# A depthwise convolution's fourth channel tile moved from TensorE to GpSimd, in a two-block transformer kernel on one core

## What is computed

```python
a, gt = jnp.split(p[..., o3:], 2, axis=-1)
u = a * jax.nn.sigmoid(gt)                        # 512 positions x 512 channels
u = _dwconv(u, w_dw_conv[l], b_dw_conv[l])        # depthwise, 31 taps along the positions, plus a bias
u = jax.nn.silu(_layernorm(u, g_conv_ln[l], b_conv_ln[l]))
y = jnp.concatenate([y_attn, u], axis=-1) @ w_o[l]
```

## Time and profile before

| | |
|---|---|
| time, median of 3 runs | 1885.44 us (1885.15 to 1885.94) |
| profiled execution, span from its first to its last instruction | 1883.8 us |
| around the span (median less span) | 1.6 us |
| busy: PE, DVE, ACT, POOL | 1861.2, 1165.4, 917.1, 75.4 us |
| granted TensorE clock, mean | 1.000 of full speed |

### The profile page before, as it was taken

One profiled execution on the slowest core, in us unless ns is written; L12 is line 12 of the kernel. 1 busy time (PEld: TensorE's weight loads), 2 busy tenths in 40 slices (PEclk: granted clock), 3 DMA queues, 4 the chain that ended last, 5 costly groups with the idle time before them and its releaser, 6 DMA issues.

```text
span 1883.8 us, 27086 instructions
## 1 busy us (share of the span) xinstructions
PE 1861.2 (99%) x8985; PEld 1504.1 (80%) x8985; DVE 1165.4 (62%) x2030; ACT 917.1 (49%) x1685; POOL 75.4 (4%) x110
## 2 busy tenths in 40 slices
PE   8999999999999999999999999999999999999998
PEld 7888888888888877677888888888757878888887
DVE  6877765733333377776566666336777576666534
ACT  6777654543433353666544434334456553444433
POOL 1111000000000000100200000000010020000000
PEclk9999999999999999999999999999999999999999
DMA  5222232333333324521333333333441223333333
GB/s 153 69 79 79 76 104 79 101 95 100 95 98 97 95 73 102 108 53 35 101 95 95 95 95 105 96 95 88 118 83 43 68 81 109 95 95 95 96 95 106
DMA packets 169241, 171.33 MB, mean 91 GB/s; under 512 B 48563, under 2 KB 123329, under 8 KB 169153
## 3 DMA queue, kind: packets, MB, share of 16 engines
q1 hardware_dynamic: 169048, 170.16, 31.5%
q10 hardware_dynamic: 104, 0.03, 0.0%
HBM read 159.25 MB, written 2.10 MB: 86 GB/s over the span
## 4 chain that ended last, share of the span: by engine, by line
PE 91%; DVE 5%; ACT 2%; issue 1%; DMA 0%; SPq 0%; DVEq 0%; ACTq 0%
PE bank_b L2457 16%; PE bank_b L2458 16%; PE bank_b L2459 16%; PE bank_a L2457 11%; PE bank_a L2458 11%; PE bank_a L2459 11%; PE bank_b L2959 2%; PE bank_b L3063 2%; PE bank_a L3044 1%; DVE w_lo L1535 1%; DVE arena L1538 1%; DVE arena L1535 1%; PE bank_a L2482 1%; PE bank_a L2485 1%; PE bank_a L2488 1%
## 5 line engine op out<-in xcount | busy, mean ns | idle before, releaser
L1535 DVE TENSOR_TENSOR w_lo<-w_raw,w_hi 128x512 fp32r<-128x512 f32 (+2 forms) x621 | 412.3, 675 | 535.3 <-ACT w_hi L1264 327.4
L1264 ACT ACTIVATE w_hi<-w_raw 128x512 fp32r<-128x512 f32 (+3 forms) x396 | 232.9, 599 | 435.6 <-PE bank_b L2459 222.2
L2457 PE MATMUL bank_b<-h_hi,w_hi 128*128 128x512 f32 (+1 forms) x952 | 372.7, 391 | 1.9 <-DVE h_lo L1538 0.8
L2459 PE MATMUL bank_b<-h_hi,w_lo 128*128 128x512 f32 (+1 forms) x952 | 369.0, 388 | 0.0
L2458 PE MATMUL bank_b<-h_lo,w_hi 128*128 128x512 f32 (+1 forms) x952 | 369.0, 388 | 0.0
L901 ACT ACTIVATE w_hi<-w_raw 128x512 fp32r<-128x512 f32 x225 | 137.7, 627 | 227.6 <-PE bank_b L2459 116.9
L2457 PEld LDWEIGHTS bank_b<-h_hi,w_hi 128*128 128x128 f32 x952 | 178.8, 188 | 41.2 <-issue 3.1
L2458 PEld LDWEIGHTS bank_b<-h_lo,w_hi 128*128 128x128 f32 x952 | 178.8, 188 | 37.0 <-issue 1.4
L2459 PEld LDWEIGHTS bank_b<-h_hi,w_lo 128*128 128x128 f32 x952 | 178.7, 188 | 36.6
L2457 PE MATMUL bank_a<-h_hi,w_hi 128*128 128x512 f32 x513 | 200.6, 391 | 0.3
L2458 PE MATMUL bank_a<-h_lo,w_hi 128*128 128x512 f32 x513 | 199.5, 389 | 0.0
(11 more groups left out here) (314 smaller groups left out, 2665.3 us busy)
## 6 DMA issues: line engine op xcount, KB each, us to landing
w_raw<-in_w_up_dram SPq DMA_DIRECT2D x240, 256.0 KB, 3.1
w_raw<-in_w_down_dram SPq DMA_DIRECT2D x152, 256.0 KB, 2.6
arena<-arena SPq DMA_DIRECT2D x32, 268.0 KB, 4.2
w_raw<-in_w_in_dram SPq DMA_DIRECT2D x64, 128.0 KB, 2.3
w_raw<-in_w_gate_dram SPq DMA_DIRECT2D x32, 256.0 KB, 2.8
w_raw<-in_w_in_dram SPq DMA_DIRECT2D x32, 256.0 KB, 2.6
w_raw<-in_w_o_dram SPq DMA_DIRECT2D x32, 256.0 KB, 2.6
w_raw<-in_w_out_dram SPq DMA_DIRECT2D x16, 256.0 KB, 2.7
```

Of the source, the lines that this page charges most:

```text
L1264: nc.scalar.activation(w_hi[:, s, 0:c], w_raw[:, s, 0:c], ACT.Copy).then_inc(w_round, 1)
L1535: return nc.vector.tensor_tensor(out_, a, b, op)
L2457: nc.tensor.matmul(out_, a_hi, b_hi, start=start, stop=False, skip_group_check=loose)
L2459: return nc.tensor.matmul(out_, a_lo, b_hi, start=False, stop=stop, skip_group_check=loose)
```

## The change

Tile 3 is no longer convolved by TensorE. Its groups, its stack, its diagonals, its three VectorE taps and its `end_conv` are gone; GpSimd does all of its 31 taps: the first as a `tensor_scalar` (times the tap, plus the bias), the other 30 as a multiply of the shifted input by the tap's column broadcast to 128x512, and an add to the running sum. The add of a tap stands behind the multiply of the next one. VectorE's `add_conv(3)` now waits for GpSimd and stands in step 24 instead of step 20.

```diff
-TILE_GROUPS = (GROUPS - 1, GROUPS - 1, GROUPS, GROUPS)
+TILE_GROUPS = (GROUPS - 1, GROUPS - 1, GROUPS, 0)
+PE_TILES = 3
+POOL_TILE = 3
-TAP_STEPS = ((), (), (1, 2, 3), (9, 10, 11))
-END_STEPS = (0, 0, 7, 12)
+TAP_STEPS = ((), (), (1, 2, 3))
+END_STEPS = (0, 0, 7)
-CONV_STEPS = ({}, {}, {3: 4, 5: 3}, {8: 4, 10: 3})
-SUM_STEPS = (8, 12, 20)
+CONV_STEPS = ({}, {}, {3: 4, 5: 3})
+SUM_STEPS = (8, 12, 24)
...
+                def pool_taps(taps):
+
+                    for k in taps:
+                        src, gain = upad[:, POOL_TILE, k:k + S], pool_gain(k)
+                        if k == 0:
+                            nc.gpsimd.tensor_scalar(pool_sum, src, gain, cols_all[:, l, L_BDW + POOL_TILE:L_BDW + POOL_TILE + 1],
+                                                    ALU.mult, ALU.add).then_inc(pool_tap, 1)
+                            continue
+                        nc.gpsimd.tensor_tensor(pool_part[k % 3], src, gain.broadcast_to((P, S)), ALU.mult).then_inc(pool_tap, 1)
+                        if k > 1:
+                            pool_add(k - 1, pool_sum, 2 * k - 2)
+
+                def pool_add(k, dst, made):
+
+                    pool.wait_ge(pool_tap, pool_at + made)
+                    nc.gpsimd.tensor_tensor(dst, pool_sum, pool_part[k % 3], ALU.add).then_inc(pool_tap, 1)
+
                 diagonals(0)
+                pool.wait_ge(pad_zero, was[pad_zero.name] + 2)
+                pool.wait_ge(u_ready, was[u_ready.name] + HT)
+                pool_taps(range(0, 8))
                 diagonals(1)
+                pool_taps(range(8, 16))
                 diagonals(2)
-                diagonals(3)
+                pool_taps(range(16, CONV_K))
+                pool_add(CONV_K - 1, conv[:, POOL_TILE, :], 2 * CONV_K - 2)
...
                 def add_conv(j):
 
-                    dve.wait_ge(conv_out, was[conv_out.name] + j + 1)
+                    if j == POOL_TILE:
+                        dve.wait_ge(pool_tap, was[pool_tap.name] + 2 * CONV_K - 1)
+                    else:
+                        dve.wait_ge(conv_out, was[conv_out.name] + j + 1)
```

More of the change, by code:

```diff
@@ L67 @@
 GROUPS = CONV_K // SHIFTS
-TILE_GROUPS = (GROUPS - 1, GROUPS - 1, GROUPS, GROUPS)
+TILE_GROUPS = (GROUPS - 1, GROUPS - 1, GROUPS, 0)
+PE_TILES = 3
+POOL_TILE = 3
 GROUPS_BEFORE = [sum(TILE_GROUPS[:j]) for j in range(len(TILE_GROUPS) + 1)]
-LAST_TAPS = range(min(TILE_GROUPS) * SHIFTS, CONV_K)
 TILE_TAPS = [CONV_K - SHIFTS * groups for groups in TILE_GROUPS]
-TAP_STEPS = ((), (), (1, 2, 3), (9, 10, 11))
-END_STEPS = (0, 0, 7, 12)
+TAP_STEPS = ((), (), (1, 2, 3))
+END_STEPS = (0, 0, 7)
 LANES = P // SHIFTS
@@ L98 @@
 L_LAST = 77
-N_ROWS2 = L_LAST + len(LAST_TAPS) * (HALF // P)
+TILE_TAP_ROW = [L_LAST + sum(TILE_TAPS[:j]) for j in range(HT)]
+N_ROWS2 = L_LAST + sum(TILE_TAPS)
 L_TAP, L_FTAP = 128, 256
@@ L208 @@
     "p_ready": (0, BLOCKS), "pt_made": (0, BLOCKS), "pt_ready": (0, BLOCKS), "v_made": (0, TT - 1), "vv_ready": (PAIRS, TT),
-    "pv_done": (0, PAIRS * TT), "conv_out": (0, HT), "conv_tap": (0, sum(TILE_TAPS)), "diag_made": (0, GROUPS_BEFORE[HT]),
+    "pv_done": (0, PAIRS * TT), "conv_out": (0, PE_TILES), "pool_tap": (0, 2 * CONV_K - 1), "conv_tap": (0, sum(TILE_TAPS[:PE_TILES])), "diag_made": (0, GROUPS_BEFORE[HT]),
     "diag_used": (0, GROUPS_BEFORE[HT]),
@@ L379, in two_blocks @@
         conv = upad[:, :, 0:S]
-        conv_part = [split_f[:, n, :] for n in (12, 13, 16, 17)]
+        conv_part = [split_f[:, n, :] for n in (12, 13, 16)]
+        pool_part, pool_sum = [split_f[:, n, :] for n in (15, 17, 20)], arena[:, 29, :]
         stacks = [arena_flat[:, first:first + 4 * STACK].rearrange("p (c n) -> p c n", c=4) for first in (18 * S, 9 * S)]
@@ L578, in two_blocks @@
         conv_tap = sem("conv_tap")
+        pool_tap = sem("pool_tap")
         conv_sum = sem("conv_sum")
@@ L595, in stacked @@
         def stacked(l, j):
-            return 16 * (P // LANES) * (2 * l + j // 2 + 1)
+            return 16 * (P // LANES) * (2 * l + j // 2 + 1 if j % 2 == 0 else l + 1)
         @block.sync
@@ L640, in _ @@
                 r += rows
-            for k in LAST_TAPS:
-                rows = HALF // P
-                sp_.dma_start(rows2[r:r + rows, :, :], w_dw_conv[:, k, :].rearrange("l (r p) -> r l p", p=P)).then_inc(rows2_land, 16)
+            for j, rows in enumerate(TILE_TAPS):
+                sp_.dma_start(rows2[r:r + rows, :, :],
+                              w_dw_conv[:, CONV_K - rows:CONV_K, j * P:j * P + P].rearrange("l k p -> k l p")).then_inc(rows2_land, 16)
                 r += rows
@@ L710, in stack_up @@
                     sp_.wait_ge(pad_zero, was[pad_zero.name] + 2)
-                    sp_.wait_ge(u_ready, was[u_ready.name] + (1, HT, HT, HT)[j])
+                    sp_.wait_ge(u_ready, was[u_ready.name] + (1, HT, HT)[j])
                     if j >= 2:
@@ L728, in _ @@
                 for i in range(PAIRS):
-                    if i >= 2:
+                    if i == 2:
                         stack_up(i)
@@ L882, in diagonals, with pool_gain @@
                                                 ALU.mult).then_inc(diag_made, 1)
+                pool_at = was[pool_tap.name]
+                def pool_gain(k):
+                    c = TILE_TAP_ROW[POOL_TILE] + k
+                    return cols_all[:, l, c:c + 1]
+                def pool_taps(taps):
[11 more added lines that the diff above has]
+                    nc.gpsimd.tensor_tensor(dst, pool_sum, pool_part[k % 3], ALU.add).then_inc(pool_tap, 1)
                 diagonals(0)
+                pool.wait_ge(pad_zero, was[pad_zero.name] + 2)
+                pool.wait_ge(u_ready, was[u_ready.name] + HT)
+                pool_taps(range(0, 8))
                 diagonals(1)
+                pool_taps(range(8, 16))
                 diagonals(2)
-                diagonals(3)
+                pool_taps(range(16, CONV_K))
+                pool_add(CONV_K - 1, conv[:, POOL_TILE, :], 2 * CONV_K - 2)
                 pool.wait_ge(stat_ready, was["stat_ready"] + 4)
@@ L2125, in _ @@
                 tap_at = was[conv_tap.name]
-                last_tap = [0] * HT
-                taps_of = [0] * HT
+                last_tap = [0] * PE_TILES
+                taps_of = [0] * PE_TILES
                 def tap(j):
                     nonlocal tap_at
-                    n = len(LAST_TAPS) - TILE_TAPS[j] + taps_of[j]
-                    k, c = LAST_TAPS[n], L_LAST + n * (HALF // P) + j
+                    k, c = CONV_K - TILE_TAPS[j] + taps_of[j], TILE_TAP_ROW[j] + taps_of[j]
                     gain = cols_all[:, l, c:c + 1]
@@ L2323, in _ @@
                             split2_lo(M_PAIR + (i + 2) * SLOTS + (2, 4, 5, 6).index(m))
-                    for j in range(HT):
+                    for j in range(PE_TILES):
                         if g in TAP_STEPS[j]:
@@ L2337, in _ @@
                 dve.wait_ge(mean_ready, was[mean_ready.name] + 1)
-                dve.wait_ge(conv_out, was[conv_out.name] + HT)
+                dve.wait_ge(conv_out, was[conv_out.name] + PE_TILES)
                 for j in range(HT):
@@ L3054, in values2 @@
                     if j == TT:
-                        pe.wait_ge(conv_out, was[conv_out.name] + HT)
+                        pe.wait_ge(conv_out, was[conv_out.name] + PE_TILES)
                     if b == 0 and i >= 2:
@@ L3102, in _ @@
                         values2((g - PV_LAG) // 2)
-                    for j in range(HT):
+                    for j in range(PE_TILES):
                         if g in CONV_STEPS[j]:
-                            if j == 3 and done[j] == 0:
-                                pe.wait_ge(conv_out, was[conv_out.name] + 3)
                             conv_taps(j, range(done[j], done[j] + CONV_STEPS[j][g]))
```

8 lines of the change are left out of this document (4 added, 4 removed).

## The result

The changed kernel takes 1964.12 us (median of four runs, 1953.87 to 1974.39), the kernel before 1885.3 us beside it: 1.0418 times as long, 95% interval 1.0388 to 1.0448. The range of 1899 to 1965 holds it by less than 1 us at its upper edge, 26 us above the predicted 1938. Two of the four runs came out near 1954 and two near 1974, the latter outside the range.

What follows compares the result with a forecast made beforehand. TensorE was taken to bound the kernel, busy 1861.2 of 1883.8 us. Per layer -6.3 + 13 + 11.5 + 8 = +26.2, twice 52.4, gave a span of 1936 and a time of 1938 us; range 1899 to 1965.

Steps and rivals of the forecast that it cites:

- The saving: Step 8 and step 10 groups taken from TensorE: 3.57 + 2.71, 6.3 us less per layer.
- Term 1: Ahead of the attention: GpSimd's first 14 instructions take turns with VectorE and make TensorE late by 13 us per layer.
- The step that named `w_lo`: Ahead of the attention: TensorE has only 0.8 us in hand for the query projection's seventh-chunk remainder.
- Term 2: Step 3: 16 GpSimd instructions delay the diagonals of tile 2, so TensorE idles 11.5 us per layer.
- The clock: TensorE at half clock behind the diagonals' wait: 3.6 us more per layer, an estimate left out of the sum.
- Term 3: Rest of the attention: the last 31 GpSimd instructions meet VectorE in steps 3 to about 20, costing 8 us per layer.
- The scalings of 0.7 us and above: Expected sign in the changed trace: VectorE's scalings this long in steps 3 to 20.
- The new wait: `add_conv(3)` in step 24: GpSimd's last add at 857, step 24 at 866, so it does not bind: 0.
- GpSimd's prices: Per 128x512 GpSimd instruction: 1.05 us for multiplies, 1.3 for adds, 1.17 on average.
- slower still: Rival, chance 0.12: a multiply by a column costs 1.62 to 2.06 us, term 2 is 18; 1971 us.

Runs made afterwards that it cites:

- experiment 1: Changed kernel without GpSimd's taps, so tile 3 is not convolved at all: 1871.45 us, 0.9927 of the kernel before.
- experiment 2: Changed kernel with only taps 0 to 7 of tile 3, ahead of the diagonals of tile 1; other taps left out: 1895.36 us, ratio 1.0054.
- experiment 4: Changed kernel with each GpSimd add right behind its own multiply and waiting for it, so gaps throughout: 1934.6 us, ratio 1.0261.
- experiment 11: Changed kernel with all 31 GpSimd taps behind the diagonals of tiles 0, 1 and 2, without gaps: 1915.12 us, ratio 1.0157.
- experiment 10: Changed kernel with eight unread VectorE additions filling its idle time before step 3's maximum; neither long idling nor long undisturbed GpSimd taps remain: 1944.01 us, ratio 1.0314.
- experiments 6 and 7: Changed kernel with tile 2's diagonals ahead of taps 8 to 30: without gaps (6) 1918.44 us; each add waiting for its multiply (7) 1916.49 us.

## Why the prediction came out as it did

**The saving.** Predicted 6.3 us per layer, 6.9 by experiment 1. Right.

**Term 1.** Predicted 13, measured 12.6 in the trace and 12.0 by experiment 2. The turns are there (a remainder of 128x384 at 1.39 us instead of 0.56, two taps in 3.23), but the total is right because errors make up for one another. VectorE lost less than the 14 us taken. The remainder of the seventh chunk, at 758.03 before, is here:

```profile
769.24 0.56 DVE L1568 TENSOR_TENSOR w_lo<-w_raw,w_hi 128x384 fp32r<-128x384 f32 x1
```

That is 11.0 us later without the 0.23, or 0.79 for each of the 14 instructions instead of 1.0. The step that named `w_lo`, with 0.8 us in hand, as what TensorE would wait for was wrong too: 9.6 come as one wait for VectorE's sum of squares (L2529), which stands behind those remainders and taps in VectorE's queue and for which TensorE had nothing in hand, since it waited 0.47 us for it already before the change; 0.6 is for `w_lo`. And 2.6 are the slower clock, which the term left out.

**Term 2.** Predicted 11.5, measured 11.9 and 12.4. Here too the parts differ: 8.0 us of waiting for the diagonals, where the text of the prediction wanted about 11; 1.6 by which TensorE comes later, which the prediction took as hidden; and 2.4 for the slower clock. The total is right partly because one part made up for another.

**The clock.** The prediction gave its price beside the sum, as an estimate of 3.6 us per layer by the Trainium skill (TensorE: Matmul & The Clock Gate, Why this matters for your kernels), and put nothing for it into the sum, since no row had a price. It measured 7.5 us per layer, behind all three waits and not behind one. A row of the kernel before could have warned, though the granted clock of its window reads 1.00: behind a wait at the start of the kernel, four transposes take 1.08 us where four in the attention take 0.60:

```profile
4.63 1.08 PE L2603 MATMUL bank_a<-ident,arena 128*128 128x128 f32 x4 [4.63 <-DMA arena<-in_x_dram]
```

**Term 3.** Here the prediction failed. Its size for turns, 8, was about right (at most 7.2, by experiment 4). The step that failed is the first one, "the last 31 instructions then run beside steps 3 to about 20": it took for granted that the two engines take turns wherever they meet, because they did so in the earlier trace rows. In the profiled executions they do not, and the term is 26.1. The meeting of the earlier trace rows had neither of the two things that the hold came with. In the kernel before, `add_squares` puts a wait for the sum directly ahead before each of GpSimd's sums after the first, so its queue has gaps, and VectorE had been idle for only 1.82 us when it came to them:

```profile
926.87 6.17 POOL L812 TENSOR_TENSOR ssum<-ssum,sq 128x512 f32<-128x512 f32 x4 [3.76 <-ACT sq L915]
```

```profile
928.91 1.28 DVE L1535 TENSOR_TENSOR w_lo<-w_raw,w_hi 128x512 fp32r<-128x512 f32 x1 [1.82 <-ACT w_hi L1264]
```

The new queue has no such waits, and term 2's wait, which the prediction had in its own sum, leaves VectorE idle for 10.8 us while GpSimd goes on; the prediction did not ask what happens when VectorE comes back. The scalings of 0.7 us and above that it expected from step 3 on are seen in the runs with turns (1.33 in experiment 4), and in the changed kernel only once behind the hold, at 851.21 (1.29).

**The new wait** at `add_conv(3)` is 0, as predicted: GpSimd is done at 852.2, far ahead of step 24, which the hold had put off. It does bind in experiment 11.

**GpSimd's prices.** Undisturbed, a multiply by a broadcast column takes 1.00 from start to start and an add 1.22 to 1.24; 1.05 and 1.3 were taken. Even the first tap, a `tensor_scalar`, takes 0.77 us in experiment 11 (1.71 in the changed kernel, beside VectorE), far below the bound of 1.62 to 2.06 that the prediction read from the earlier trace rows. The rival *slower still* has with 1971 nearly the time of the profiled execution, by causes that are not there: no multiply at 1.6 us, no term 2 of 18.

**The median** of 1964 is the middle between two kinds of execution, near 1954 and near 1974, and no execution took it. That it lies within the range is luck: the six executions near 1974, of eight, lie above 1965. Without the hold, in experiment 4, the kernel takes 1934.6 us, so the mechanism that was predicted gives about the predicted 1938, if with parts that make up for one another.

## What to carry to other kernels

Before GpSimd gets work beside a busy VectorE, count what an instruction of its costs there: here 0.85 us ahead of the attention (12.0 / 14, the slower clock behind the wait included) and 0.25 to 0.36 in it (47 and 61 instructions, experiments 6 and 11), against TensorE's 6.9 us for all 61 instructions, so none of the orders tried made it pay, and 61 times 0.25 is more than 6.9 as well. What other engines wait for (the diagonals) goes ahead of the new work in GpSimd's queue, since such a wait costs more than its own length (9.1 us for 8.1). A long GpSimd queue of instructions with two SBUF operands should have a wait for the instruction directly ahead in it now and then, above all where VectorE returns from a wait: one such wait was worth 18 us per layer against the longer executions. A wait of TensorE is charged with the slower matmuls behind it, here 2.4 to 2.6 us each.

## What the runs showed of the hardware that was not expected

A VectorE instruction that needs 0.42 us was held for 27.8 to 28.1 us in all six layers profiled of the changed kernel, across some 25 GpSimd instructions, and let go at GpSimd's first gap. It was let go after 3.7 us with one gap put in, not held with gaps all along, and not held without gaps if VectorE had been at work until then or idle for up to 3.7 us. The Trainium skill (SBUF — State Buffer, SBUF: two separate sides) gives the shared port pair to whichever of the two engines starts first, for the whole instruction, and has the other blocked. One instruction at a time fits the turns in kind (1.10 us per sum of 1.29) and not the hold; that GpSimd keeps the pair until its queue has a gap would fit the hold and not the turns, which occur in queues without gaps too. Both occur here, and what decides is shown only as far as these runs go: which of the two conditions of experiment 10 it is, how long VectorE must have been idle, and whether the executions near 1954 lack one of the holds, stays open.

The way in which the two engines meet also fixed what turns cost: 0.25 us per GpSimd instruction in the attention, where VectorE has room, with or without the gaps (experiments 6 and 7).
